# Delta setup of a two-block kernel: work ordered by pairs, block products in whole phases with projection steps between

## The chip, the cores and the metric

The kernel runs on one core of one Trainium2 chip. The metric is the device time of one execution in microseconds. TensorE (PE), VectorE (DVE), ScalarE (ACT), GpSimd (POOL) and SyncE (SP, which only issues DMAs here) run side by side and wait for one another by semaphores.

## What is computed

Four mixers over 256 tokens of width 1024, all in fp32: a gated delta rule layer, an attention layer with a relative bias, a retention layer and a chunked attention layer. The change is in the first, before its output projection:

```
proj = hn @ w_in                                  # q, k, v, z and the gates
qkv  = silu(causal_conv(proj_qkv, conv_w))        # 4 taps
g = cumsum(g); decay = exp(g_i - g_j) below the diagonal, else 0
a_mat = strict_lower((k * beta) @ k.T * decay)
u, w  = solve((a_mat + I), [v * beta, k * beta * exp(g)])
o     = scan over chunks with u, w, q, k, decay
```

In the last two mixers a modulation is needed as well: `mod = silu(c) @ ada_w + ada_b`, 6144 values, read as 24 pairs of columns of 128 (1 MB of weights each).

## The kernel before

**Projections.** Every projection is cut into jobs of 256 columns. A job takes one weight chunk of 1 MB (a job of the third and fourth output projection takes two), which SP loads into `raw` (three buffers: chunk c is issued when the low part of chunk c - 3 is done). ScalarE rounds it to its high part (`high(c)`, two halves, L980), DVE subtracts to get the low part (`low(c)`, two halves, L1382), and PE multiplies three times per tile (high by high, high by low, low by high). `parts(J, s0, s1)` does steps s0 to s1 of the eight steps of job J; a step is six matmuls of 128x256. Two PSUM banks alternate between jobs.

**Delta setup.** Jobs 0 to 7 give keys and queries, 8 to 11 the values, 12 to 15 the gate z. From job 8 on they are cut up and laid between the setup of the delta rule, in an order that is written out by hand on each engine. For each of four pairs of heads p: `decay_rows(p)` spreads the rows of g over the partitions, `masked(p)` adds the causal mask, `products(p, 0)` and `products(p, 1)` make k k' and q k'. ScalarE makes `state_decay(p)` and `decay(p)` (L1108, L1117), DVE multiplies them in `pair_matrices(p)` (L1531 to L1535) into `nt` and `qkd`.

The inverse of the unit lower triangle is then built in seven levels. In levels 0 to 4 `first_products` and `second_products` are 64 block matmuls of 32x32 each (128 rows in the trace), with a ScalarE copy between them (L1154). `take_rows` on DVE puts the results into the triangle (L1552) and transposes it (L1556). Level 5 joins blocks of 32, level 6 blocks of 64. Between the phases PE does four steps of a job, the transposes of the keys (level 1) and of the values (levels 2 to 5), and in levels 5 and 6 a modulation sum. Values that have been transposed are scaled into `vr` by DVE (`take_values`, L1487).

**Modulation.** For pair n DVE multiplies and adds the 1 MB ring of weights (`pair_sums(n)`, L1460 to L1467), PE sums over the partitions (`ada(n)`, two matmuls of one column), DVE adds the bias (`take_mod`, L1473). `ADA_AT[n]` is the job of pair n; the next pair's weights are loaded into the ring three chunks after it. Pairs 0 to 2 are in the setup or just behind it.

**Bias rows.** POOL writes two tables of bias rows to DRAM, each row 32 times (`scr_d` 1 MB and `scr_b` 0.5 MB, L426 and L428), to be read back skewed for the two attention layers.

PE then takes the delta rule's chain (`un_ok` to `o_ok`), the output projection (jobs 16 to 19) and the other mixers, in jobs 20 to 103.

Of the kernel before, what the change touches and what calls it, by code (L numbers as in the profile page):

```python
# [15 lines left out]
P = 128  # L16
# [10 lines left out]
ALU = mybir.AluOpType  # L27
# [35 lines left out]
ADA_AT = [13, 14, 15, 25, 27, 29, 31, 33, 35, 42, 44, 46, 48, 50, 52, 54, 56, 58, 60, 62, 78, 82, 86, 90]  # L63
ADA_EARLY = 3
# [11 lines left out]
def two_blocks(nc, x_in, wts, ada_w, cols_in, const_in, lmask_in, w_ab, rel_b, rel_d, dtab, pos, out,  # L76
               scr_b, scr_d):
    ctx = ExitStack()
    with ctx:  # L79
# [120 lines left out]
        for lv in range(1, LEVELS):  # L200
            if lv == LEVELS - 1:
                turn_order += [f"level{lv}_{g}" for g in range(4)]
            if 2 <= lv <= 5:
                turn_order.append(f"values{lv - 2}")
            if lv >= 5:
                turn_order.append(f"mod{lv - 5}")
# [182 lines left out]
        def _(pool):  # L389
# [35 lines left out]
            pool.wait_ge(nt_ok_sem, 4)  # L425
# [49 lines left out]
        def _(pe):  # L475
# [58 lines left out]
            def ada_after(J):  # L534

                for n in range(ADA_EARLY, ADA_PAIRS):
                    if ADA_AT[n] == (J + 3 if J >= JOB_D else J):
                        if J >= JOB_D:
                            pe.wait_ge(pT_v_sem, 2 * (4 + (J - JOB_D) // 4))
                        pe.wait_ge(mod_ok_sem, n - 2)  # L540
                        ada(n)
# [88 lines left out]
            pe.wait_ge(const_r_sem, 3)  # L630
            decay_rows(0)
# [18 lines left out]
            def first_products(lv, c0):  # L650

                left = left_of(lv) if lv < 5 else lambda v: v
                n = 16 if lv < 5 else 32
                for m16 in range(16):
                    o = slice(c0 + m16 * n, c0 + m16 * n + n)
# [4 lines left out]
            def second_products(lv, c0):  # L660

                n = 16 if lv < 5 else 32
                for m16 in range(16):
                    o, i = slice(c0 + m16 * n, c0 + m16 * n + n), slice(m16 * n, m16 * n + n)
# [7 lines left out]
            parts(9, 4, 8)  # L672
# [7 lines left out]
            for lv in range(1, LEVELS):  # L680
                J = 9 + lv
# [31 lines left out]
                if lv >= 5:  # L713
# [91 lines left out]
            ada(ADA_EARLY - 1)  # L805
# [24 lines left out]
            def attend(J0, pairs, soft0, o0, h_q, h_kv, normed, ready, extra):  # L830
                def turn(i):
                    pe.wait_ge(p_soft_sem, soft0 + i + 1)
                    if soft0 == 0:
                        pe.wait_ge(ss_read_sem, own_ss[0])
                    for hh in range(2):
                        if soft0 == 4 and hh and 1 <= i < 5:
                            pe.wait_ge(mod_ok_sem, 18 + i)
# [126 lines left out]
        def _(act):  # L964
# [155 lines left out]
            state_decay(0)  # L1120
            state_decay(1)
            high(9)
            decay(0)
            decay(1)
            first_tap(8)
            state_decay(2)
            state_decay(3)
            decay(2)
            decay(3)
            high(10)  # L1130
            silu(8)
# [6 lines left out]

            for lv in range(1, LEVELS):
                J = 9 + lv  # L1140
                high(J + 1)
                if lv == LEVELS - 1:
# [7 lines left out]
                else:  # L1150
                    act.wait_ge(x_ok_sem, lv)
                    n = 256 if lv < 5 else 512
                    for k, r in steps_of(lv):
                        m = act.activation(xs32[block_of(r), 0:n], ps[2 + k][block_of(r), 0:n], ACT.Copy)  # L1154
                    m.then_inc(xc_ok_sem, 1)
                    if lv == 5:
                        act.wait_ge(t_ok_sem, 5)
                        act.wait_ge(tt_ok_sem, 5)
                        for i in range(4):
                            m = act.activation(tt[block_of(i), :, block_of(i)], tt32[block_of(i), :, :], ACT.Copy)  # L1160
                        m.then_inc(tt_diag_sem, 1)
                if J - 1 < 12:
                    first_tap(J - 1)
                else:
                    gate_z(J - 1)
                if lv in (2, 3, 4):
                    silu(J - 2)
                if lv >= 2:
                    for p in ((lv - 2,) if lv < 6 else ()):
                        act.activation(qsq[:, 2 * p:2 * p + 2, :], qh[:, 2 * p:2 * p + 2, :], ACT.Square, scale=0.128).then_inc(qsq_ok_sem, 1)  # L1170
# [185 lines left out]
        def _(dve):  # L1356
# [9 lines left out]
            def low(c, halves=range(2)):  # L1366

                if c >= N_CHUNKS:
                    return
                low_only(c, halves)  # L1370
                if c in ADA_AT[ADA_EARLY:]:
                    n = ADA_AT.index(c)
                    if ADA_EARLY < n < 20:
                        take_mod(n - 1)
                    pair_sums(n)
# [104 lines left out]
            def take_values(i):  # L1480

                b, free, n = slot(slot_of_values(i))
                dve.wait_ge(vT_ok_sem, i + 1)
                for c in range(2):
                    for hh in range(2):
                        k = 8 * c + 2 * i + hh
                        m = dve.tensor_scalar(vr[:, 4 * i + 2 * c + hh, :], b[:, (2 * c + hh) * P:(2 * c + hh) * P + P], hc[:, 4, k:k + 1], None, ALU.mult)  # L1487
                m.then_inc(free, 1)

# [47 lines left out]
            low(9)  # L1537
            pair_matrices(0)
            pair_matrices(1)
            conv(8)  # L1540
# [26 lines left out]
            low(10)  # L1567
            for lv in range(1, LEVELS - 1):
                low(10 + lv)
                if lv == 1:  # L1570
# [7 lines left out]
                    dve.wait_ge(ce_sem, 2)  # L1578
                else:
                    take_values(lv - 2)  # L1580
# [4 lines left out]
                if lv <= 3:  # L1585
                    conv(8 + lv)
                if lv == 4:
                    dve.wait_ge(sil_ok_sem, 1)
                    pair_sums(0)
                if lv == 5:  # L1590
                    mod_of_slot(0)
                    pair_sums(1)
            mod_of_slot(1)
            pair_sums(2)
# [141 lines left out]

            add_x(JOB_OUT_A, before_last=lambda: take_mod(ADA_EARLY - 1))

# [31 lines left out]
            def gains_of_c():  # L1770
                for n in range(ADA_EARLY - 1):
                    dve.wait_ge(slot(slot_of_mod(n))[1], slot(slot_of_mod(n))[2] + 1)
                dve.wait_ge(mod_ok_sem, 6)
# [72 lines left out]
            dve.wait_ge(mod_ok_sem, 10)  # L1846
            add_x(JOB_OUT_C, gate=16, before_last=lambda: take_mod(19))
            dve.wait_ge(mod_ok_sem, 18)
# [9 lines left out]
            dve.wait_ge(mod_ok_sem, 22)  # L1858
# [118 lines left out]
```

## Time and profile before

| | us |
|---|---|
| median of 3 runs | 860.55 (859.98 to 864.71) |
| profiled execution | 857.89 |
| its span in the profile | 856.0 |
| TensorE busy in the span | 827.2 (97%) |
| VectorE, ScalarE, GpSimd busy | 602.2, 484.0, 42.0 |
| granted TensorE clock, mean | 0.986 of 2.4 GHz |

The span is the stretch that the profile shows; the profiled execution took 1.9 us more than it. The granted clock of 1.00 is 2.4 GHz, 0.50 is 1.2 GHz. A busy PE is not PE at its peak.

### The profile page before, as it was taken

To read this page: it belongs to the slowest core of one execution; us is meant where nothing else is said; L and a number is where in the kernel's file an instruction comes from. 1 tells how busy PE (TensorE), PEld (TensorE's weight loads), DVE (VectorE), ACT (ScalarE), POOL (GpSimd) and SP (SyncE) were. 2 spreads that over 40 slices of the span, in tenths; PEclk is the share of its full clock that TensorE was granted. 3 is DMA by queue.
4 is the path that set the end of the run, shared out by engine and by line. 5 is a ranking of instruction groups with operands and counts; after the bars stand their busy time and mean duration, and the time that the engine had idled before them with its cause. 6 is when DMAs were issued, how large, how long until landed. Compare 5 with 4: busy or idle time off the path is not lost. (4 is left out here: it accounts for less than half of the span.)

```text
span 856.0 us, 18089 instructions
## 1 busy us (share of the span) xinstructions
PE 827.2 (97%) x7682; PEld 804.6 (94%) x7682; DVE 602.2 (70%) x1058; ACT 484.0 (57%) x746; POOL 42.0 (5%) x63
## 2 busy tenths in 40 slices
PE   6999879899999999999999999998999999999998
PEld 6899878898999999999999999998999999999998
DVE  5785667667887877596888885646678677565662
ACT  4765435445666564564454445345867767777731
POOL 4100000003600000000000000200000000000000
PEclk9999889899999999999999999999999999999999
DMA  7363371261876565447666564793456444434350
GB/s 279 111 242 129 51 188 58 102 221 57 237 236 245 199 244 198 148 154 281 217 234 238 210 244 147 198 289 123 179 197 224 166 156 178 163 119 177 133 188 25
DMA packets 26497, 153.84 MB, mean 180 GB/s; under 512 B 2848, under 2 KB 3376, under 8 KB 12080
## 3 DMA queue, kind: packets, MB, share of 16 engines
q1 hardware_dynamic: 24432, 146.37, 48.3%
q0 software_dynamic: 1984, 6.31, 4.2%
q8 instruction: 61, 1.00, 0.4%
q14 instruction: 20, 0.16, 0.1%
HBM read 150.04 MB, written 2.62 MB: 178 GB/s over the span
## 5 line engine op out<-in xcount | busy, mean ns | idle before, releaser
L1382 DVE TENSOR_TENSOR wlo<-raw,whi 128x1024 fp32r<-128x1024 f32 x224 | 266.1, 1225 | 128.8 <-ACT whi L980 128.8
L479 PE MATMUL ps<-hhi,whi 128*128 128x256 f32 x1024 | 297.3, 290 | 7.4 <-DVE hlo L1408 4.4
L980 ACT ACTIVATE whi<-raw 128x1024 fp32r<-128x1024 f32 x224 | 227.0, 1053 | 126.9 <-PE ps L479 87.5
L479 PE MATMUL ps<-hlo,whi 128*128 128x256 f32 x1024 | 292.6, 286 | 2.7 <-issue 2.7
L479 PE MATMUL ps<-hhi,wlo 128*128 128x256 f32 x1024 | 292.3, 285 | 1.0 <-issue 1.0
L479 PEld LDWEIGHTS ps<-hhi,whi 128*128 128x128 f32 x1024 | 198.7, 194 | 10.7 <-issue 6.4
L479 PEld LDWEIGHTS ps<-hlo,whi 128*128 128x128 f32 x1024 | 198.9, 194 | 3.4 <-issue 2.9
L479 PEld LDWEIGHTS ps<-hhi,wlo 128*128 128x128 f32 x1024 | 198.8, 194 | 1.2 <-issue 1.2
L479 PE MATMUL ps<-ohi,whi 128*128 128x256 f32 x448 | 128.8, 287 | 1.3 <-DVE olo L1427 1.2
L479 PE MATMUL ps<-ohi,wlo 128*128 128x256 f32 x448 | 126.7, 283 | 0.0
L479 PE MATMUL ps<-olo,whi 128*128 128x256 f32 x448 | 126.7, 283 | 0.0
L479 PEld LDWEIGHTS ps<-ohi,whi 128*128 128x128 f32 x448 | 85.9, 192 | 2.4 <-issue 1.6
L479 PEld LDWEIGHTS ps<-olo,whi 128*128 128x128 f32 x448 | 85.9, 192 | 0.5 <-issue 0.5
L479 PEld LDWEIGHTS ps<-ohi,wlo 128*128 128x128 f32 x448 | 85.9, 192 | 0.0
L479 PE MATMUL ps<-arena 128*128 128x256 f32 (+2 forms) x496 | 77.8, 308 | 0.7 <-ACT arena L1343 0.7
L479 PEld LDWEIGHTS ps<-arena 128*128 128x128 f32 (+1 forms) x496 | 70.1, 191 | 7.1 <-issue 3.0
L479 PE MATMUL ps<-whi,hhi 128*128 128x256 f32 x256 | 72.8, 284 | 0.0
L479 PE MATMUL ps<-whi,hlo 128*128 128x256 f32 x256 | 72.4, 283 | 0.0
L479 PE MATMUL ps<-wlo,hhi 128*128 128x256 f32 x256 | 72.4, 283 | 0.0
L1463 DVE SCALAR_TENSOR_TENSOR ada_ring<-ada_ring,sil 128x256 f32<-128x256 f32 x144 | 59.0, 477 | 0.0
L479 PEld LDWEIGHTS ps<-whi,hhi 128*128 128x128 f32 x256 | 49.0, 191 | 0.7 <-issue 0.4
L479 PEld LDWEIGHTS ps<-whi,hlo 128*128 128x128 f32 x256 | 49.0, 191 | 0.3
(221 smaller groups left out, 967.7 us busy)
## 6 DMA issues: line engine op xcount, KB each, us to landing
raw<-weights SPq DMA_DIRECT2D x112, 1024.0 KB, 4.9
ada_ring<-ada SPq DMA_DIRECT2D x24, 1024.0 KB, 5.0
arena<-bias_rows_d POOLq DMA_DIRECT2D x4, 512.0 KB, 15.1
x<-x_t SPq DMA_DIRECT2D x2, 512.0 KB, 4.6
bias_rows_d<-early POOLq DMA_DIRECT2D x1, 1024.0 KB, 12.0
arena<-bias_rows_b POOLq DMA_DIRECT2D x4, 256.0 KB, 7.5
arena<-bias_rows_d POOLq DMA_DIRECT2D x4, 256.0 KB, 17.9
out_t<-x SPq DMA_DIRECT2D x4, 256.0 KB, 2.9
```

The source lines that it names most:

```text
L479: return pe.matmul(o, l, r, start=start, stop=stop, skip_group_check=skip)
L980: act.activation(whi[:, unit % UNITS, :, :], raw[:, c % RAW, 4 * half:4 * half + 4, :], ACT.Copy).then_inc(hi_ok_sem, 1)
L1382: dve.tensor_tensor(wlo[:, unit % UNITS, :, :], raw[:, c % RAW, 4 * half:4 * half + 4, :], whi[:, unit % UNITS, :, :].bitcast(F32), ALU.su ...
L1463: own(dve.scalar_tensor_tensor(out=b, in0=b, scalar=sil[:, k:k + 1], in1=ring[:, :, k - 2, :], op0=ALU.mult, op1=ALU.add))
```

## The change

1. The order of the decay and product matmuls goes by pairs: each mask follows the first product of its pair. ScalarE makes state decay and decay of a pair together.
2. Projection steps are counted by `weave`, which goes on from where it stopped: nine steps before level 0, three behind it, and nine in each of the levels 1 to 6 (four behind the first products, five behind the second). The sum is 66; the last two belong to chunk 16, whose bank the output projection begins anew.
3. ScalarE's and DVE's high and low parts, first taps, silus and gates are placed by level to fit. The low part of chunk 9 stands behind the first two pairs of matrices.
4. The values are scaled into `vr` by ScalarE instead of DVE.
5. One modulation pair is left in the setup (level 6); the two others get the jobs 23 and 66, and the waits and indices follow.
6. The two writes of the bias rows wait for the second first tap instead of the last pair of matrices.

```diff
-ADA_AT = [13, 14, 15, 25, 27, 29, 31, 33, 35, 42, 44, 46, 48, 50, 52, 54, 56, 58, 60, 62, 78, 82, 86, 90]
-ADA_EARLY = 3
+ADA_AT = [14, 23, 25, 27, 29, 31, 33, 35, 42, 44, 46, 48, 50, 52, 54, 56, 58, 60, 62, 66, 78, 82, 86, 90]
+ADA_EARLY = 1
...
-            pool.wait_ge(nt_ok_sem, 4)
+            pool.wait_ge(tap_ok_sem, 2)
             pool.dma_start(scr_d[0:32].rearrange("p h t -> h p t"), fd[:, :].unsqueeze(1).to_broadcast([16, 32, 512])).then_inc(scr_out_sem, 16)
...
+            def weave(n):
+                for _ in range(n):
+                    parts(8 + woven[0] // 8, woven[0] % 8, woven[0] % 8 + 1)
+                    woven[0] += 1
             decay_rows(0)
             decay_rows(1)
             products(0, 0)
+            masked(0)
             products(0, 1)
             products(1, 0)
-            parts(8, 0, 4)
+            masked(1)
+            weave(2)
             products(1, 1)
-            masked(0)
-            masked(1)
-            parts(8, 4, 8)
-            for p in (2, 3):
-                decay_rows(p)
-                products(p, 0)
-                products(p, 1)
-            parts(9, 0, 2)
+            weave(2)
+            decay_rows(2)
+            products(2, 0)
             masked(2)
+            products(2, 1)
+            weave(2)
+            decay_rows(3)
+            products(3, 0)
             masked(3)
-            parts(9, 2, 4)
+            products(3, 1)
+            weave(3)
...
             first_products(0, 256).then_inc(tp_ok_sem, 1)
-            parts(9, 4, 8)
+            weave(3)
...
-                if lv >= 5:
-                    ada(lv - 5, taken(slot_of_mod(lv - 5)))
-                parts(J, 0, 4)
                 if last:
+                    ada(0, taken(slot_of_mod(0)))
+                    weave(4)
...
+                    weave(5)
                 else:
+                    weave(4)
                     pe.wait_ge(xc_ok_sem, lv)
                     pe.wait_ge(u32_ok_sem, lv)
                     second_products(lv, 256 if lv < 5 else 0).then_inc(tp_ok_sem, 1)
-                parts(J, 4, 8)
+                    weave(5)
...
-            ada(ADA_EARLY - 1)
...
             for lv in range(1, LEVELS):
+                if 2 <= lv <= 4:
+                    first_tap(7 + lv)
+                elif lv >= 5:
+                    gate_z(7 + lv)
+                if lv < LEVELS - 1:
+                    high(9 + lv, range(1))
+                    act.wait_ge(x_ok_sem, lv)
...
+                    high(9 + lv, range(1, 2))
+                    if lv >= 2:
+                        take_values(lv - 2)
+                    if lv <= 4:
+                        silu(7 + lv)
+                    if lv == 5:
...
+                        high(15)
...
-            low(9)
             pair_matrices(0)
             pair_matrices(1)
-            conv(8)
+            low(9)
             pair_matrices(2)
             pair_matrices(3)
...
             take_rows(0)
-            low(10)
+            conv(8)
             for lv in range(1, LEVELS - 1):
-                low(10 + lv)
+                if 2 <= lv <= 4:
+                    conv(7 + lv)
+                low(9 + lv)
...
-            mod_of_slot(1)
-            pair_sums(2)
+            low(15)
+            dve.wait_ge(sil_ok_sem, 1)
+            pair_sums(0)
+            mod_of_slot(0)
```

## Rows read from the trace of the kernel before

**Rows 1.** The page: busy us (share of the span) and instructions of PE.

```profile
PE 827.2 (97%) x7682; PEld 804.6 (94%) x7682; DVE 602.2 (70%) x1058; ACT 484.0 (57%) x746; POOL 42.0 (5%) x63
```

**Rows 2.** Windows by stage: length, then busy us of each engine, PEclk, DMA share, GB/s.

```profile
73.30:98.80 25.50, 22.96 (x157) 20.83 (x156) 13.88 (x31) 13.05 (x33) 0.00 (x0) 0.93 0.23 83
98.80:181.00 82.20, 72.45 (x1706) 68.51 (x1707) 56.45 (x116) 35.49 (x60) 1.41 (x2) 0.88 0.48 129
...
200.00:856.00 656.00, 647.60 (x5189) 637.49 (x5188) 465.28 (x795) 377.28 (x560) 27.44 (x33) 1.00 0.55 189
```

**Rows 3.** Waits of PE in the setup, 73 to 181 us: total, times, longest.

```profile
PE ps L479 <- issue: 7.7, 5, 2.7
PE ps L479 <- DVE arena L1535: 2.6, 1, 2.6
PE ps L479 <- DVE ada_sum L1467: 1.3, 1, 1.3
```

**Rows 4.** Windows before one fall of the clock and in two stretches behind falls.

```profile
95.40:98.85 3.45, 0.89 (x12) 0.69 (x10) 2.96 (x7) 3.43 (x9) 0.00 (x0) 1.00 0.00 0
98.85:105.70 6.85, 6.85 (x151) 6.81 (x152) 4.75 (x7) 2.73 (x3) 1.41 (x2) 0.50 0.73 82
...
119.30:126.10 6.80, 6.59 (x149) 6.33 (x150) 5.19 (x11) 3.61 (x8) 0.00 (x0) 0.51 0.58 196
```

**Rows 5.** Timeline of PE: start, us, operation, count, idle before it.

```profile
87.86 2.05 PE L479 MATMUL ps<-arena 128*128 128x128 f32 x16
...
105.94 1.26 PE L479 MATMUL ps<-early,arena 32*32 32x16 f32 x128
...
119.51 0.58 PE L479 MATMUL ps<-hlo,whi 128*128 128x256 f32 x1 [2.69 <-issue]
...
134.41 0.38 PE L479 MATMUL ps<-hhi,whi 128*128 128x256 f32 x1 [0.24 <-DVE early L1449]
...
137.47 0.71 PE L479 MATMUL ps<-early 32*32 32x16 f32 x64
```

**Rows 6.** Timeline of ACT.

```profile
54.66 2.01 ACT L980 ACTIVATE whi<-raw 128x1024 fp32r<-128x1024 f32 x2
57.27 0.63 ACT L1064 ACTIVATE arena<-arena 128x512 f32<-128x512 f32 x1 [0.60 <-DVE arena L1449]
...
78.44 0.64 ACT L1108 ACTIVATE early<-ps 128x256 f32<-128x256 f32 x2
```

**Rows 7.** Timeline of DVE.

```profile
100.87 2.96 DVE L1552 COPY_PREDICATED early<-lmask,ps 32x256 f32<-32x256 uint8 x4 [2.10 <-PE ps L479]
...
154.03 2.46 DVE L1463 SCALAR_TENSOR_TENSOR ada_ring<-ada_ring,sil 128x256 f32<-128x256 f32 x6
...
246.10 2.35 DVE L1382 TENSOR_TENSOR wlo<-raw,whi 128x1024 fp32r<-128x1024 f32 x2
...
543.12 0.87 DVE L1666 SCALAR_TENSOR_TENSOR x<-ps,mod,x 128x256 f32<-128x256 f32 x2
```

**Rows 8.** POOL's write; the software queue in 106 to 110 us; landings, 98 to 130 us.

```profile
99.41 0.71 POOL L426 DMA_DIRECT2D bias_rows_d<-early  x1 [64.58 <-DVE arena L1535]
...
q0 software_dynamic: 101, 0.41, 96.7%
...
raw<-weights SPq DMA_DIRECT2D x1, 1024.0 KB, 17.4
...
bias_rows_d<-early POOLq DMA_DIRECT2D x1, 1024.0 KB, 12.0
bias_rows_b<-early POOLq DMA_DIRECT2D x1, 512.0 KB, 21.9
```

**Rows 9.** DMA queues in 549 to 571 us: packets, MB, share of the engines.

```profile
q1 hardware_dynamic: 522, 3.88, 70.6%
q0 software_dynamic: 530, 1.86, 30.6%
```

**Rows 10.** Waits of ACT, 540 to 580 us.

```profile
ACT whi L980 <- DMA raw<-weights: 10.4, 5, 4.0
```

More of the change, by code:

```diff
@@ L204, in two_blocks @@
                 turn_order.append(f"values{lv - 2}")
-            if lv >= 5:
-                turn_order.append(f"mod{lv - 5}")
+            if lv == 6:
+                turn_order.append("mod0")
         turn_order += [f"sum{i}" for i in range(4)]
@@ L633, in _, with first_products @@
             products(0, 0)
+            masked(0)
             products(0, 1)
             products(1, 0)
-            parts(8, 0, 4)
+            masked(1)
+            weave(2)
             products(1, 1)
-            masked(0)
-            masked(1)
-            parts(8, 4, 8)
-            for p in (2, 3):
-                decay_rows(p)
-                products(p, 0)
-                products(p, 1)
-            parts(9, 0, 2)
+            weave(2)
+            decay_rows(2)
+            products(2, 0)
             masked(2)
+            products(2, 1)
+            weave(2)
+            decay_rows(3)
+            products(3, 0)
             masked(3)
-            parts(9, 2, 4)
-            def first_products(lv, c0):
+            products(3, 1)
+            weave(3)
+            def first_products(lv, c0, between=()):
                 left = left_of(lv) if lv < 5 else lambda v: v
@@ L654, in first_products @@
                 for m16 in range(16):
+                    if m16 in between:
+                        weave(1)
                     o = slice(c0 + m16 * n, c0 + m16 * n + n)
@@ L658, in first_products, with second_products @@
                 return m
-            def second_products(lv, c0):
+            def second_products(lv, c0, between=()):
                 n = 16 if lv < 5 else 32
                 for m16 in range(16):
+                    if m16 in between:
+                        weave(1)
                     o, i = slice(c0 + m16 * n, c0 + m16 * n + n), slice(m16 * n, m16 * n + n)
@@ L836, in turn @@
                         if soft0 == 4 and hh and 1 <= i < 5:
[L837 removed]
+                            pe.wait_ge(mod_ok_sem, 19 + i)
                         if soft0 + i:
@@ L1120, in _ @@
             state_decay(0)
+            decay(0)
             state_decay(1)
+            decay(1)
             high(9)
-            decay(0)
-            decay(1)
+            state_decay(2)
+            decay(2)
+            state_decay(3)
+            decay(3)
             first_tap(8)
[L1126 to L1131, printed above, removed]
             def gate_z(J):
@@ L1137, in gate_z, with take_values @@
                 act.activation(zt[:, 2 * i:2 * i + 2, :], bank(J), ACT.Silu).then_inc(bank_free[J % 2], 1)
-            for lv in range(1, LEVELS):
-                J = 9 + lv
-                high(J + 1)
-                if lv == LEVELS - 1:
+            def take_values(i):
+                b, free, n = slot(slot_of_values(i))
+                act.wait_ge(vT_ok_sem, i + 1)
+                act.wait_ge(ce_sem, 2)
+                for c in range(2):
+                    for hh in range(2):
+                        k = 8 * c + 2 * i + hh
+                        m = act.activation(vr[:, 4 * i + 2 * c + hh, :], b[:, (2 * c + hh) * P:(2 * c + hh) * P + P], ACT.Copy, scale=hc[:, 4, k:k + 1])
+                m.then_inc(free, 1)
+            for lv in range(1, LEVELS):
+                if 2 <= lv <= 4:
[5 more added lines that the diff above has]
+                    act.wait_ge(x_ok_sem, lv)
+                    n = 256 if lv < 5 else 512
+                    for k, r in steps_of(lv):
+                        m = act.activation(xs32[block_of(r), 0:n], ps[2 + k][block_of(r), 0:n], ACT.Copy)
+                    m.then_inc(xc_ok_sem, 1)
+                    high(9 + lv, range(1, 2))
[4 more added lines that the diff above has]
+                    if lv == 5:
+                        act.wait_ge(t_ok_sem, 5)
+                        act.wait_ge(tt_ok_sem, 5)
+                        for i in range(4):
+                            m = act.activation(tt[block_of(i), :, block_of(i)], tt32[block_of(i), :, :], ACT.Copy)
+                        m.then_inc(tt_diag_sem, 1)
+                        high(15)
+                else:
                     for g in range(4):
@@ L1149, in _ @@
                         act.activation(uu[:, 4 * g:4 * g + 4, :], v2(b, P), ACT.Copy).then_inc(free, 1)
[L1150 to L1170, printed above, removed]
+                    gate_z(14)
+                    high(16)
+                if 2 <= lv <= 5:
+                    p = lv - 2
+                    act.activation(qsq[:, 2 * p:2 * p + 2, :], qh[:, 2 * p:2 * p + 2, :], ACT.Square, scale=0.128).then_inc(qsq_ok_sem, 1)
             for p in range(4):
@@ L1372, in low @@
                     n = ADA_AT.index(c)
-                    if ADA_EARLY < n < 20:
+                    if ADA_EARLY < n < 20 and n != 8:
                         take_mod(n - 1)
@@ L1478, in mod_of_slot @@
                 take_mod(n, b, free)
[L1480 to L1488, printed above, removed]
             dve.wait_ge(ones_ok_sem, 6)
@@ L1735, in attend @@
                 finish(pairs - 1)
-            add_x(JOB_OUT_A, before_last=lambda: take_mod(ADA_EARLY - 1))
+            add_x(JOB_OUT_A)
             low(JOB_B + 1, range(1, 2))
@@ L1770, in gains_of_c @@
             def gains_of_c():
-                for n in range(ADA_EARLY - 1):
-                    dve.wait_ge(slot(slot_of_mod(n))[1], slot(slot_of_mod(n))[2] + 1)
-                dve.wait_ge(mod_ok_sem, 6)
+                take_mod(7)
+                dve.wait_ge(slot(slot_of_mod(0))[1], slot(slot_of_mod(0))[2] + 1)
+                dve.wait_ge(mod_ok_sem, 7)
                 scaled_gain(0)
@@ L1845, in _ @@
             finish_c(3, 1)
-            dve.wait_ge(mod_ok_sem, 10)
+            dve.wait_ge(mod_ok_sem, 11)
             add_x(JOB_OUT_C, gate=16, before_last=lambda: take_mod(19))
-            dve.wait_ge(mod_ok_sem, 18)
+            dve.wait_ge(mod_ok_sem, 19)
             scaled_gain(1)
@@ L1857, in _ @@
             attend(JOB_D, 8, 4, A(bias_at, 16, 384), True)
-            dve.wait_ge(mod_ok_sem, 22)
+            dve.wait_ge(mod_ok_sem, 23)
             add_x(JOB_OUT_D, gate=40)
```

16 lines of the change are left out of this document (2 added, 14 removed).

## The prediction

> **What bounds the kernel now.** I first read the page's busy shares: PE is busy for 97% of the span [rows 1]. Next I cut the span into stages. From 200 us on PE is busy for 647.6 of 656 us at full clock; the delta setup, 73.3 to 181.0, is where it is neither (2.5 us idle in the first part, 9.8 us in the second, granted clock 0.93 and 0.88) [rows 2]. The waits of PE there say what the idle time is: 7.7 us under "issue", 2.6 us for the last decay matrices, 1.3 us for the first modulation sum [rows 3]. The windows around the clock's changes show the rest: three times it stands at 1.2 GHz for 6.8 us, each time after PE had waited beside small products (0.9 us busy of 3.45 before the first) [rows 4] (two are shown, the third lies at 156.9 to 163.7). So PE's own order sets the end, and a change here is worth what it removes in idle time and in stretches at 1.2 GHz.
>
> **A model of the setup, tested on the kernel before.** From the timeline of PE [rows 5]: a block of 24 projection matmuls (4 steps of `parts`) takes 3.06 us (134.41 to 137.47), so a step is 0.765; a phase of 128 block products takes 1.19 (1.26 shown) at full clock, 1.9 at half; eight products of 128x128 take 2.05, so one call of `products` is 1.03. The 52 steps after 98.82 make 39.8 us, nine phases and the two of level 5 make 13.2, the transposes, the 64-wide products and the two modulation sums 11.1: 64.1 us, which would end at 162.9. The setup ends at 180.9. The missing 18.0 are 7.7 of issue stalls, 1.5 of other waits, and 8.8, or 2.9 for each of the three times at 1.2 GHz.
>
> **Order by pairs.** The new order begins `masked(0)` right after `products(0, 0)`, at about 77.1. It needs the first state decay, which ScalarE finishes at 78.8 [rows 6]; what stood in that gap, two calls of products, now stands behind it. PE waits 1.8 us. From there I add four masks (0.3 each), seven calls of products, two of decay rows (0.53 each) and nine steps: the first level can start near 95.3, with `nt_ok` 4 reached at 94.5 (the last `decay` is 1.1 us, the last pair of matrices 1.4). Before, it started at 98.8 with 12 steps done: 3.5 us earlier, less 2.3 us for the three steps still to do. The 2.6 us wait goes.
>
> **Levels.** There are nine steps in each level where there were eight, 57 to the end of the setup. Counted, 12 + 54 is 66 steps where jobs 8 to 15 have 64: two surplus steps, 12 matmuls, are paid with 1.4 us. 57 steps make 43.6, the rest 23.9 (one modulation sum less): 67.5 us. To this come waits. After level 0 only three steps (2.3 us) cover the four masked copies of 2.96 us [rows 7]: 0.8. VectorE then has a convolution (2.4), a low part (2.35) and the scaled keys (2.2) before the copies of level 1: 0.7. From level 2 on VectorE has 7.3 us of work (the values went to ScalarE) in a level of 9.9. At level 5 ScalarE now does 1.2 + 1.1 + 1.1 (values) + 2.55 + 2.0 + 0.6 and then the gate of job 13, which job 15 waits for: 9.2 us after the products, where PE arrives after 8.1: 1.1. With 0.2 more the waits are 2.8, and the setup would end at 165.6. I choose this small sum for the values on ScalarE because its four copies have the size of those that VectorE does in 1.12; nothing in the trace lets ScalarE's differ by more than a few tenths.
>
> **What comes back of stalls and clock.** The stalls named issue [rows 3] stand 127 or 128 matmuls apart where one follows another (three such pairs in the timeline; the stall of the first ends at 119.51 [rows 5]). I read them as a fetch of the next piece of program, which from stall's end to stall's end takes 3.7 to 4.1 us, and 5.9 to 7.2 while the bias rows were being written. In the new order I counted on in steps of 127: four of twelve pieces last only 2.3 to 3.6 us. That makes some 5 us of stalls; the bounds are 3 and 8. The clock: the likeliest place for a fall is the wait before level 2 with its first products and a stall behind them, then the waits at levels 5 and 6. I take between one and two falls, 4 us; bounds 0 and 8.8 (as before). So the setup ends at 174.6, 6.3 us earlier: I take 6 us gained, between 2 and 13.
>
> **Bias rows in the first jobs.** The two writes of 1.5 MB move from 99.4 to about 35.0 (the second first tap ends at 34.5, the filled rows at 34.8) [rows 6, 8]. In their old place they took 12.0 and 21.9 us to land, and the weight chunk issued 7.4 us behind them took 17.4 [rows 8]: in 106 to 110 us the software queue held 96.7% of the DMA engines and the weights' queue moved nothing, and from 111 to 122 it still held half. That chunk was not needed for 20 us. In the new place chunk 6 is issued at 41.2, 6.2 us behind the writes; in the same way it would land at about 60. ScalarE takes it at 54.66 in the trace of before, ahead of the silu and the squares of job 4 (0.63 + 0.63) [rows 6], and PE's key sums at 60.02 wait for those squares. So: 59.8 + 2.0 + 1.3 gives 63.2, a wait of 3.2 us, 5.6 if the writes are late by the 2.3 us that chunk 5 still needs. I take 3.5. The lower bound is nothing: the later bias load shares, weights 70.6% and software queue 30.6% [rows 9], and then chunk 6 lands near 50. The upper is 7.6: chunk 5, issued at 34.24, is held as well and its low part, due at 54.2, comes at 61.8. The Trainium skill's page DMA: Bandwidth & Descriptors, section Queues, rings and completion order, says that each engine takes turns between the queues that have work, a packet at a time; by it this term would be nothing. No weights moved in 106 to 110, so this trace speaks against it for these writes.
>
> **Modulation sums at jobs 23 and 66.** Each moves 3.5 us of VectorE (0.6 + 2.46 + 0.42) [rows 7] and 0.4 of PE out of the setup; PE's part is the same in sum. At chunk 23 they stand before the eight low parts of h and the low part of chunk 24: this ended at 248.4, its first half at 247.3, and job 24 begins at 249.3. Now the half comes at 250.9: 1.2 us, and 0.3 again at job 26, whose low part follows the softmax that is 2.5 us later. I take 1.5 (bounds 0.5 and 2.5). At chunk 66 they stand before the update of x at 543.1, whose square on ScalarE is ahead of the high part of chunk 67: low part at 550.5 instead of 546.9, due at 548.1, 2.4 us. And the ring's next MB is now loaded at chunk 69 (about 546.7), not at 65, into 541 to 577 us, where the DMA engines are full and ScalarE already waits 10.4 us for weights [rows 9, 10]. One MB is 2.5 to 5 us there; since the end of this stage hangs on the last weights before too, the two don't add. I take 3.0 (bounds 1.5 and 5).
>
> **Sum.** -6 + 3.5 + 1.5 + 3.0 = +2 us on the profiled execution's 857.9, so 859.9; the median of the runs shown stands 2.7 above that execution, so 862.5. What this kernel's measurement can tell from no change is 0.5%, or 4.3 us.
>
> **Rivals.** (a) The clock does not fall in the new setup and the stalls lie in the waits: 13 us gained, -5, and 852 to 856 by how many of the other terms are paid. For it: the projection steps now stand in every level between the phases, and the longest wait left is 1.8 us. Against it: each of the three falls of before followed such a meeting [rows 4]. It decides from 12.3 us gained in the setup. 0.14. (b) The queues share, the bias rows cost nothing (the page's rule): -1.5, 859. Only with more than 9 us gained in the setup is that faster. 0.23. (c) Chunk 5 is held with chunk 6: +6, 866.6. 0.14. (d) The clock falls three times as before, once after the 1.8 us wait at 77, so that the setup gives 1 to 2 us: +6.5, 867. 0.14. My forecast: 0.35.
>
> **Chances and range.** Faster: all of (a) and 0.07 of (b): 0.21. Slower: (c), (d) and 0.06 of the forecast's own upper end: 0.34. The same: 0.45. The range takes in (a)'s upper half and (d) with a stall more: 854 to 870; the forecast's own is 858 to 866.
>
> **What would show it.** No wait of 2.6 us before the first phase, and a wait of 1.8 near 77; 12 matmuls more on PE; the setup's end between 172 and 178, with issue stalls of 3 to 8 us; the landing time of chunks 5 and 6, and PE waiting at key sums near 60 for ScalarE's squares; a wait for a low part at the start of job 24; waits for low parts in jobs 65 and 67. I am wrong if chunk 6 lands by 50, if the clock is full from 82 to the end of the setup or falls three times in it, or if the low parts of 24, 67 and 70 come in time.

## The result, and the profile after

The changed kernel takes 864.43 us in the median of 20 runs (860.88 to 868.83), the kernel before 860.28 in the same number (854.79 to 865.11). The ratio is 1.0052, with a 95% interval of 1.0029 to 1.0075: slower by half a per cent, just at the edge of what a measurement of this kernel tells from no change. The profiled execution has a span of 862.2 us against 856.0, 6.2 more. The medians are 4.2 apart: the profiled execution of the kernel before (857.89) lies 2.4 below its median, that of the changed kernel (864.05) 0.4 below.

The page of the changed kernel has the 12 surplus matmuls, and 1.2 us more of PE time with them, against [rows 1]:

```profile
PE 828.4 (96%) x7694; PEld 805.9 (93%) x7694; DVE 598.8 (69%) x1042; ACT 487.4 (57%) x762; POOL 41.9 (5%) x63
```

**Where the 6.2 us are.** Four marks on PE cut both traces: the key sums of job 7 (72.43 before, 77.29 after), the first inner products behind the setup (180.88, 177.00), the last sums of x's squares behind job 70 (577.14, 584.74), and the end. The start costs 4.9 us. The setup takes 99.7 us and no longer 108.5, which gives 8.7. The stretch from there to the x sums takes 407.7 and no longer 396.3, which costs 11.5, and 1.4 come back behind it, where PE before waited 1.1 us. 4.9 - 8.7 + 11.5 - 1.4 is 6.2 with the rounding.

The start. POOL writes the bias rows 64 us earlier than in [rows 8]; the software queue in 40 to 44 us, and the landings in 30 to 70 us:

```profile
35.09 0.71 POOL L426 DMA_DIRECT2D bias_rows_d<-early  x1 [0.31 <-POOL early L423]
...
q0 software_dynamic: 101, 0.41, 94.5%
...
bias_rows_d<-early POOLq DMA_DIRECT2D x1, 1024.0 KB, 12.8
...
bias_rows_b<-early POOLq DMA_DIRECT2D x1, 512.0 KB, 23.0
```

In 40 to 44 us the queue of the weights has no row at all, as in 106 to 110 before. Chunk 6 was issued at 41.14; its first packet moved at 45.50, 4.4 us later, where before it was 1.0 us (42.16 after 41.20). From 48 to 55 us the two queues moved side by side, the software queue with 48.3% of the engines and the weights with 37.7%. ScalarE gets chunk 6 at 60.06, where [rows 6] has 54.66, and PE's key sums wait for the squares behind it. The timelines of ACT and of PE, and two windows of PE's clock:

```profile
60.06 2.00 ACT L993 ACTIVATE whi<-raw 128x1024 fp32r<-128x1024 f32 x2 [5.34 <-DMA raw<-weights]
...
62.62 0.63 ACT L1082 ACTIVATE early<-arena 128x512 f32<-128x512 f32 x1
```

```profile
63.30 1.05 PE L479 MATMUL ps<-ones,early 128*128 128x1 f32 x8 [3.17 <-ACT early L1082]
...
83.72 0.80 PE L479 MATMUL ps<-causal_r,ident_r 128*128 128x512 f32 x1 [2.47 <-ACT early L1121]
...
102.25 1.26 PE L479 MATMUL ps<-early,arena 32*32 32x16 f32 x128
...
106.67 1.26 PE L479 MATMUL ps<-early,arena 32*32 32x16 f32 x128 [0.82 <-DVE early L1568]
...
120.23 0.27 PE L479 MATMUL ps<-hhi,wlo 128*128 128x256 f32 x1 [0.68 <-issue]
125.56 0.36 PE L479 MATMUL ps<-early 32*32 32x16 f32 x20 [1.89 <-issue]
```

```profile
65.00:71.00 6.00, 6.00 (x41) 6.00 (x41) 4.18 (x11) 1.50 (x2) 0.00 (x0) 0.75 0.65 246
82.00:88.00 6.00, 4.28 (x18) 4.19 (x19) 1.87 (x5) 3.04 (x10) 0.00 (x0) 0.50 0.00 0
125.50:131.00 5.50, 5.44 (x50) 5.41 (x49) 4.92 (x12) 0.00 (x0) 0.00 (x0) 0.69 0.26 100
```

Behind the wait of 3.17 us the clock falls to half for part of 65 to 71 us; that is the rest of the 4.9. In the setup it falls twice more, once about the wait of 2.47 for the first state decay (82 to 88 us) and once behind the stall of 1.89 (125.5 to 131), where it fell three times before.

The setup from mark to mark, the kernel before first, the changed one second (each an answer of its own trace; the columns are those of [rows 2]):

```profile
72.40:180.90 108.50, 96.22 (x1871) 90.14 (x1870) 70.27 (x148) 49.21 (x93) 1.41 (x2) 0.89 0.41 117
```

```profile
77.30:177.00 99.70, 90.53 (x1878) 84.94 (x1877) 60.71 (x112) 53.02 (x109) 0.00 (x0) 0.95 0.28 97
```

The idle time goes from 12.3 to 9.2 us, and PE is busy 5.7 us less for seven matmuls more, because the clock is 0.95 and no longer 0.89.

Jobs 64 to 68. PE's timeline shows the two waits for low parts; the windows behind each show the clock; DVE and ACT show what was late:

```profile
547.88 0.39 PE L479 MATMUL ps<-ohi,whi 128*128 128x256 f32 x1 [1.96 <-DVE wlo L1409]
...
570.46 0.55 PE L479 MATMUL ps<-ohi,whi 128*128 128x256 f32 x1 [3.23 <-DVE wlo L1409]
```

```profile
545.00:550.00 5.00, 3.04 (x23) 2.83 (x22) 3.40 (x3) 4.41 (x5) 0.00 (x0) 0.93 1.00 219
550.00:555.00 5.00, 5.00 (x34) 5.00 (x34) 1.23 (x2) 0.00 (x0) 0.00 (x0) 0.73 1.02 244
...
570.00:575.00 5.00, 4.54 (x21) 4.57 (x22) 3.42 (x6) 2.53 (x4) 1.84 (x2) 0.50 0.92 352
575.00:580.00 5.00, 5.00 (x38) 5.00 (x37) 2.47 (x3) 1.83 (x2) 0.00 (x0) 0.84 0.61 218
```

```profile
541.26 2.44 DVE L1490 SCALAR_TENSOR_TENSOR ada_ring<-ada_ring,sil 128x256 f32<-128x256 f32 x6
...
544.08 0.87 DVE L1675 SCALAR_TENSOR_TENSOR x<-ps,mod,x 128x256 f32<-128x256 f32 x2
546.60 3.50 DVE L1409 TENSOR_TENSOR wlo<-raw,whi 128x1024 fp32r<-128x1024 f32 x3 [1.65 <-ACT whi L993]
```

```profile
568.00 2.00 ACT L993 ACTIVATE whi<-raw 128x1024 fp32r<-128x1024 f32 x2 [9.15 <-DMA raw<-weights]
```

The first wait is the chain of the prediction: pair 19's sums, the update of x, its square, the high part of chunk 67, its low part. The second is the last weight chunk of the stage, which lands late behind the ring's load (issued at 544.19). The waits are 5.2 us. The clock takes 1.7 us in 545 to 555 (0.07 and 0.27 of 5 us each) and 3.3 us in 570 to 580. That makes 10.2 (0.5 us of idle time at 570 us is counted in both), and from the start of job 64 to the x sums it is 53.6 us where the kernel before needed 43.4, which is 10.2 as well. With the 1.4 us that come back behind the x sums these jobs cost 8.8. The other 1.3 us of the stretch were lost earlier, in jobs 16 to 63.

### The profile page after: what moved, and what is told of

Read it like the earlier page. It is cut to its first block, busy times and chain, and to the rows that moved or that the text cites. A ratio compares the mean times of both kernels' runs of the same rounds, so it can differ in the third digit from the quotient of the medians.

```text
span 862.2 us, 18118 instructions
## 1 busy us (share of the span) xinstructions
PE 828.4 (96%) x7694; PEld 805.9 (93%) x7694; DVE 598.8 (69%) x1042; ACT 487.4 (57%) x762; POOL 41.9 (5%) x63
## 4 chain that ended last, share of the span: by engine, by line
PE 83%; DVE 6%; DMA 5%; ACT 4%; issue 2%; SPq 0%; DVEq 0%; ACTq 0%
PE ps L479 81%; DMA raw<-weights 5%; DVE wlo L1409 1%; ACT whi L993 1%; PE ps L854 1%; DVE early L1568 1%; ACT L982 0%; DVE early L1441 0%; DVE hlo L1435 0%; DVE hlo L1437 0%; DVE arena L1441 0%; DVE early L1476 0%; ACT arena L1182 0%; DVE arena L1476 0%; DVE ada_ring L1490 0%
## 5 line engine op out<-in xcount | busy, mean ns | idle before, releaser
L479 PE MATMUL ps<-ohi,whi 128*128 128x256 f32 x448 | 130.9, 292 | 6.5 <-DVE wlo L1409 5.2
L479 PE MATMUL ps<-ohi,wlo 128*128 128x256 f32 x448 | 128.6, 287 | 0.0
L479 PE MATMUL ps<-olo,whi 128*128 128x256 f32 x448 | 128.6, 287 | 0.0
L479 PEld LDWEIGHTS ps<-ohi,whi 128*128 128x128 f32 x448 | 87.9, 196 | 8.1 <-issue 5.1
L479 PEld LDWEIGHTS ps<-olo,whi 128*128 128x128 f32 x448 | 87.9, 196 | 0.5 <-issue 0.5
L479 PEld LDWEIGHTS ps<-ohi,wlo 128*128 128x128 f32 x448 | 87.8, 196 | 0.0
```

The lines of the kernel that those rows point to most:

```text
L479: return pe.matmul(o, l, r, start=start, stop=stop, skip_group_check=skip)
```

## The experiments

The prediction was near in time, but it had taken the setup's gain for the order's and the bias writes for a loss alone, and the stage of jobs 64 to 68 cost three times its term. Each kernel below is the changed kernel with one edit, unless it says otherwise. Each was timed in five rounds against the kernel before; the ratio is to that kernel (the changed one stands at 1.0052).

**e1, the bias writes in their old place.**

```
-            pool.wait_ge(tap_ok_sem, 2)
+            pool.wait_ge(nt_ok_sem, 4)
```

> The changed kernel with the two bias writes back behind the last pair of matrices. Theory (the writes held weight chunk 6): chunk 6 lands within 6 us of its issue, the wait of 3.17 us at the key sums near 60 goes, and job 7 no longer runs at 1.2 GHz (1.7 us), so the key sums of job 7 start at 72.4 instead of 77.3, 4.9 us earlier. Part of it is given back in the setup, where two fetch stalls get 1.5 to 3 us longer: 2 to 3.5 us faster than the changed kernel in all, ratio to the kernel before about 1.002. Rival (ScalarE's own order makes the key sums late): the wait stays and the time is that of the changed kernel.

867.82 us, ratio 1.0097 (1.0062 to 1.0132): 3 to 4 us slower than the changed kernel and not 2 to 3.5 faster. The start is back (key sums at 60.87 and 73.28), but the setup takes 113.2 us. (Its profiled execution was the slowest of its ten, 873.5.) PE's timeline, then the software queue and the instruction queue in 106 to 110 us:

```profile
112.12 0.94 PE L479 MATMUL ps<-early,arena 32*32 32x16 f32 x55 [8.32 <-issue]
```

```profile
q0 software_dynamic: 242, 0.39, 89.7%
q8 instruction: 1, 0.02, 1.5%
```

For 8.3 us PE stands in the middle of a phase with no semaphore to wait for, while the bias writes hold the DMA engines. In its setup the stalls named issue are 14.0 us, where the changed kernel has 3.7.

What PE waited for can be read from the instruction queue. From 98.5 to 109.5 us the software queue is the only one with packets:

```profile
q0 software_dynamic: 297, 1.05, 87.8%
```

The instruction queue has none there; then one of 16,384 bytes moves from 109.75 to 110.74, and PE goes on at 112.12. It is so with every stall named issue in the setups of all fourteen traces of this case, 48 of them: each ends 1.2 to 1.6 us behind the end of such a packet. And each stands at a fixed place of the program, whatever work lies there: counted in matmuls from the kernel's start, the places are multiples of 127.3 apart (978 in the kernel before and in e1, 1360 in the changed kernel and in e1, 1997 in all fourteen). So these stalls are PE's wait for the next piece of its program, and the bias writes make them longer by holding that piece back.

**e5, the same wait moved in the kernel before, nothing else.**

```
-            pool.wait_ge(nt_ok_sem, 4)
+            pool.wait_ge(tap_ok_sem, 2)
```

> The kernel before with nothing changed but the place of the two bias writes (behind the second first tap). Theory: key sums of job 4 and 5 wait 3.2 us for ScalarE, the key sums of job 7 start 4.9 us later than before; in the setup the stalls of 2.3 and 2.7 us shrink to about 1 each and one fall of the clock may go with them (2.9 us). In all 0 to 3 us slower, ratio 1.000 to 1.003. Rival (the writes cost nothing where they are): the key sums of job 7 stay at 72.4 and the kernel is 2 to 6 us faster than before.

856.80 us, ratio 0.9956 (0.9924 to 0.9989): the one line makes the old kernel faster, where the theory had 0 to 3 us slower. The start costs 7.3 us here (key sums at 64.22 and 79.70; against the changed kernel's 4.9, 1.1 more are a fall of the clock near 20 us, which some executions have, and 1.5 a longer fall behind the wait), and the setup then takes 98.0:

```profile
79.70:177.70 98.00, 88.72 (x1870) 83.00 (x1869) 70.06 (x148) 49.19 (x93) 0.00 (x0) 0.97 0.32 113
```

Put together, the setup from mark to mark is:

| | old order | new order |
|---|---|---|
| bias writes at 98 to 99 us | 108.5 | 113.2 (e1) |
| bias writes at 35 to 36 us | 98.0 (e5) | 97.0 to 102.6 (five executions: the changed kernel and e2, e3, e4, e9) |

Down the columns it is 10.5 us, and 10.6 to 16.2. Along the second row it is nothing that five executions with a spread of 5.6 us can tell. The other three cells are one execution each, e1's the slowest of ten and the two of the old order faster than their medians by 2.4 and 2.5 us. If the whole difference between an execution and its kernel's median lay in the setup, the old order would stand at 110.8 and 100.5 us, e1 at 107.5 and the changed kernel at 100.1. By this estimate the late writes cost 10.3 us in the old order and 7.4 in the new, and the new order gives 0.4 to 3.3 us, which the intervals of about 3 us on each side do not tell from nothing. So the gain in the setup belongs in the main to the bias writes, and the new order has none that is shown, though it has two pairs of modulation sums less to do.

**e6, the bias writes behind level 5** (`pool.wait_ge(t_ok_sem, 6)`; they are issued at 153.0).

> The changed kernel with the bias writes behind the halves of level 5 (near 158 us), where the next weight chunk is not needed for over 20 us and PE has few small products left. Theory: the 4.9 us at the start come back and the setup keeps its 8.7 us, so 4 to 5 us faster than the changed kernel, ratio to the kernel before 0.999 to 1.001. Rival (writes cost the same wherever they lie, by contention with the fetches): stalls in level 6 and behind it take 3 us or more back.

856.33 us, ratio 0.9976 (0.9945 to 1.0008). That is more than the 4 to 5 us expected, and both halves are had: the start of before (61.07 and 73.48) and a setup of 96.6 us. Its issue stalls are 2.6 us, none of them behind the writes, so the rival falls: the writes do not cost the same wherever they lie. The setup ends at 170.1, 6.9 us before the changed kernel's. The stretch behind it is still 407.9 us, with a wait of 6.0 at the last weight chunk in place of 3.2, and 6.7 of the 6.9 us are there at the x sums.

**e7, the masks later.** `masked(0)` stands behind the third call of products and `masked(1)` behind the first two steps.

```
             products(0, 0)
-            masked(0)
             products(0, 1)
             products(1, 0)
-            masked(1)
+            masked(0)
             weave(2)
+            masked(1)
             products(1, 1)
```

> The changed kernel with the first mask behind the third call of products and the second mask behind two steps, nothing else moved. Theory (the 2.47 us wait for the first state decay is the price of putting the mask first, and the clock stays at 1.2 GHz for it): the wait shrinks to under 0.3 us, the first block products start 2 to 4 us earlier against the key sums of job 7, and the kernel is that much faster than the changed one, ratio to the kernel before about 1.002. Rival (decay of pair 0 then comes later and the wait moves to the products of pair 2): the start of the first block products moves by less than 1 us.

861.36 us, ratio 1.0028 (1.0000 to 1.0056). The wait of 2.47 is 0.7, the first block products start 21.3 us behind the key sums of job 7 and no longer 25.0, the clock is full through the whole setup, and the setup takes 93.8 us, less than any of the five in the table. The key sums of job 7 come late in this execution (80.06), so that the spans differ by 3.0. In the medians it is 3 us as well, and the intervals of the two kernels overlap.

**e2, pair 19 at chunk 64 in place of 66** (its ring load goes to 67).

```
-ADA_AT = [14, 23, 25, ..., 60, 62, 66, 78, 82, 86, 90]
+ADA_AT = [14, 23, 25, ..., 60, 62, 64, 78, 82, 86, 90]
```

> The changed kernel with modulation pair 19 at job 64 instead of 66; the ring load of pair 20 then is issued two chunks earlier, before the late bias load begins. Theory (the 8.8 us lost in jobs 64 to 68 come from this pair's place): the waits of 1.96 and 3.23 us for low parts and the two falls of the clock behind them go; 6 to 8 us faster than the changed kernel, ratio to the kernel before 0.996 to 0.998. Rival (the loss comes from the shifted phase of the late bias load, not from the pair): both waits stay.

859.47 us, ratio 1.0007 (0.9977 to 1.0037). That is 4 to 5 us below the changed kernel, where 6 to 8 were expected. Both waits for low parts are gone, and a new one stands earlier, for the low part of the attention's output, which VectorE now does behind the sums (the timelines of PE and of DVE):

```profile
525.10 4.52 PE L479 MATMUL ps<-arena 128*128 128x256 f32 x16 [4.07 <-DVE olo L1454]
```

```profile
519.33 2.46 DVE L1490 SCALAR_TENSOR_TENSOR ada_ring<-ada_ring,sil 128x256 f32<-128x256 f32 x6
...
524.26 0.69 DVE L1454 TENSOR_TENSOR olo<-arena,ohi 128x512 fp32r<-128x512 f32 x1
```

**e3, only the ring's load later** (for pair 20 at chunk 74; pair 19 stays at 66).

```
-  if c == (ADA_AT[n - 1] + 3 if n else 8):
+  if c == ((74 if n == 20 else ADA_AT[n - 1] + 3) if n else 8):
```

> The changed kernel with only the ring load of pair 20 moved from chunk 69 to chunk 74, behind the late bias load. It tells the two causes in jobs 64 to 68 apart. If the ring load fills the DMA engines (my second cause), the wait of 3.23 us for the low part of chunk 70 and the fall behind it go, 4 to 6 us faster than the changed kernel; the wait of 1.96 us for chunk 67 stays. If all comes from the sums on VectorE, both waits stay within 0.5 us.

857.74 us, ratio 0.9973 (0.9941 to 1.0005). The second wait is gone, the first is the same, with the clock behind it (the timeline of PE and a window):

```profile
545.30 0.39 PE L479 MATMUL ps<-ohi,whi 128*128 128x256 f32 x1 [1.96 <-DVE wlo L1409]
```

```profile
545.00:550.00 5.00, 4.70 (x26) 4.71 (x27) 3.65 (x4) 1.83 (x2) 0.00 (x0) 0.66 1.01 256
```

The stretch from the setup to the x sums is 401.7 us instead of 407.7: 6.0 less for one load of 1 MB that is issued 25 us later.

**e4, only pair 19's sums later on VectorE** (behind the low parts of chunks 67 and 68; the ring's load stays at 69).

```
-  if c in ADA_AT[ADA_EARLY:]:
+  if c in ADA_AT[ADA_EARLY:] and c != 66:
...
+  if J0 == JOB_OUT_C and n == 1:
+      take_mod(18)
+      pair_sums(19)
```

> The changed kernel with only the sums of pair 19 on VectorE moved from before the update of x after job 64 to behind the low parts of chunks 67 and 68; the ring load stays at chunk 69. If the order on VectorE is the first cause, the wait of 1.96 us for the low part of chunk 67 goes (and with it the fall behind it, 1.5 us) and the wait of 3.23 us for chunk 70 stays or grows to 5: 0 to 3 us faster than the changed kernel. If the ring load is the cause of both waits, both stay.

864.51 us, ratio 1.0069 (1.0037 to 1.0101): nothing gained in the median. The first wait is gone and the second is longer:

```profile
575.00 0.55 PE L479 MATMUL ps<-ohi,whi 128*128 128x256 f32 x1 [6.51 <-DVE wlo L1409]
```

The stretch is 406.2 us, 1.5 less. While the last chunk is late, what is saved ahead of it is waited for there.

**e9, e3's and e4's edits together.**

> Changed kernel with both edits of the two runs before: the ring's load for pair 20 is issued at chunk 74 and pair 19's sums stand behind the low parts of chunks 67 and 68. Theory (each of the two waits of jobs 65 and 67 has its own cause, and the cost of the stage is the waits and the clock falls behind them): the ring's load was the larger part (its removal alone gave 6 to 8 us), and the sums only move a wait from chunk 67 to the last weight chunks (their removal alone gave nothing). With the load out of the way the sums no longer stand between a late chunk and its low part: both waits go, and the time is 1 to 3 us below the ring edit alone, 855 to 857. Rival (the sums cost VectorE 3.5 us wherever they stand in these jobs, and the end of the stage hangs on VectorE's low parts): within 1 us of the ring edit alone, 857 to 859, with one wait of 2 us at a later chunk.

856.88 us, ratio 0.9983 (0.9955 to 1.0011). No wait of 1 us or more is left from 540 to 577 us, and the stretch is 398.0 us: 9.7 less than the changed kernel, where the two edits alone gave 6.0 and 1.5. The median is 0.9 us below e3's, which is less than its interval; the trace agrees with the theory, and the medians decide nothing between it and the rival.

**e10, the values on VectorE again.** The four scaled copies of `take_values` are VectorE's `tensor_scalar` as before the change, ahead of `take_rows` in levels 2 to 5.

> Changed kernel with the values copied by VectorE again, everything else as in it. Theory (ScalarE is the late one at level 5, by 1.35 us, and VectorE's copies of levels 1 to 4 have room for 1.12 us more): the wait at level 5 goes, the other levels wait 0 to 1.1 us longer where VectorE has a low part and a convolution; the sum within 1.5 us of the changed kernel, 863 to 866, so that the move of the values is worth nothing that can be measured. Rival (VectorE is what sets each level of the new order, and the move is what made the order possible): each of levels 2 to 4 waits about 1 us and the clock falls behind one or two of them; 867 to 872.

863.36 us, ratio 1.0049 (1.0014 to 1.0085), the same as the changed kernel's. The wait at level 5 is 0.35 us, not 1.35, and the other levels wait 1.4 us where the changed kernel's wait 1.1. The setup takes 97.9. The rival, that this move made the order possible, falls.

**e8, e6 + e7 + e2 and two surplus steps fewer** (`weave(3)` at the end).

> The changed kernel with four edits together: bias writes behind level 5, pair 19 at job 64, the first masks later, and no surplus steps. Theory: 4.5 + 7 + 2 + 1.4 = 15 us faster than the changed kernel, ratio to the kernel before 0.986 to 0.991. Rival (the gains share the same falls of the clock and fetch stalls, so they don't add): 6 to 9 us faster than the changed kernel, ratio 0.994 to 0.998.

850.69 us, ratio 0.9901 (0.9867 to 0.9935): by the ratios 13.0 us faster than the changed kernel, where the theory said 15 and the rival 6 to 9. Alone e6, e2 and e7 gave 6.5, 3.9 and 2.1 us by their ratios, 12.5 in sum, so with the two surplus steps gone the gains add within their intervals.

**e11, the same with e3's edit in place of e2's.**

> The version with the bias writes behind level 5, the masks later and two surplus steps fewer, but with pair 19 left at chunk 66 and the ring's load for pair 20 issued at chunk 74 (in place of the pair at chunk 64). Theory (the pair at chunk 64 costs a wait of 4.1 us for the output's low part that the ring edit does not have, and keeps clear of the two waits of jobs 65 and 67; the ring edit leaves only the wait of 2 us): 1 to 2 us below the version with the pair at 64, 848 to 850. Rival (the two are alike, both end with the last weight chunk): within 1 us of it, 850 to 852.

846.45 us (six runs), ratio 0.9872 (0.9830 to 0.9913). It lies below the expected 848 to 850. Its profiled execution was the slowest of the six (850.8), and even so its span of 849.0 is 1.4 below e8's; the stretch takes 400.2 us against e8's 403.1. By the trace the edit to the ring is the better of the two, and the intervals of e8 and e11 overlap.

**e12, e11 with e4's edit as well.**

> The fastest version so far (bias writes behind level 5, masks later, two surplus steps fewer, the ring's load for pair 20 at chunk 74) with pair 19's sums moved behind the low parts of chunks 67 and 68 as well. In the profiles, the stretch from the first inner products behind the setup (near 171 to 181 us) to the last sums of x's squares (near 577) takes 407.7 us in the changed kernel, 401.7 with the ring edit, 398.0 with ring and sums edits together, 396.3 in the kernel before. Theory (the stretch is set by PE's order and its two waits there, whatever the setup did before it): 396 to 398 us here too, where the version without the move of the sums takes 400.2, so 2 to 4 us less in the span, 845 to 847, and a median of 843 to 846. Rival (what the stretch gives back is taken elsewhere, or the medians can't tell it): the same 400 us and a median of 846 to 848.

845.74 us (six runs), ratio 0.9844 (0.9809 to 0.9879), the fastest kernel here, though its median can't be told from e11's. The profiled execution was its fastest, with a span of 841.5. The stretch takes 398.4 us (e11: 400.2), so 1.8 of the 7.5 us between the two spans (e11's slowest execution against e12's fastest) are the edit's; 5.2 are the setup, which is the same code in both (e12 first, e11 second):

```profile
73.20:165.60 92.40, 86.93 (x1866) 81.43 (x1865) 60.24 (x112) 53.03 (x109) 1.42 (x2) 0.98 0.39 104
```

```profile
73.60:171.30 97.70, 91.50 (x1867) 85.69 (x1866) 60.40 (x113) 53.23 (x109) 1.42 (x2) 0.93 0.39 103
```

## Why the prediction was right or wrong

The forecast was 862.5 us, its own range 858 to 866, and the median is 864.4. Against the kernel before it was +2; the medians have +4.2, the trace +6.2.

**The setup: 6 forecast, 8.7 measured, with the wrong cause.** The parts that could be read off the trace came as worked out: 57 + 9 steps and 12 matmuls more, waits of 0.82 and 0.31 after levels 0 and 1 (0.8 and 0.7 forecast), 1.35 at level 5 (1.1), 3.7 us of stalls (5), the setup's end at 177.0, in the forecast's 172 to 178. The step that failed is the reading of what comes back of stalls and clock. I took the three falls of before for the meeting of waits with small products, which the order would mend, and the bias writes only for a load on the weights' queue. e5 has the old order with its phases unmended, and without the writes in it the setup takes 98.0 us. The trace of before had said as much: pieces of program took 3.7 to 4.1 us, and 5.9 to 7.2 while the bias rows were being written. I used that row for a part of the stalls and did not ask what the whole setup would be without the writes. That the setup's gain came out near its term is luck: the order, which the term was for, has 0.4 to 3.3 us by the estimate under e5.

**The wait for the first state decay** was 2.47 us, not 1.8, and the clock stood at half around it. In e7 the wait is 0.7 and the clock stays full, so both were a cost of putting the mask first.

**The bias rows in the first jobs: 3.5 forecast, 4.9 measured.** The mechanism held to the tenth: chunk 6 at 60, key sums at 63.2 against 63.30, 3.17 us of wait. What was left out is the fall of the clock behind the wait. Rival (b), that the bias rows cost nothing, falls: chunk 6 landed 18.9 us after its issue, and even its first packet moved only 4.4 us after it. The prediction's reading of 106 to 110 us was too strong, though: the weight chunk was issued only at 106.85, and its first packet moved at 110.57. The Trainium skill's page DMA: Bandwidth & Descriptors, section Queues, rings and completion order, lets each engine take turns between queues, a packet at a time. The 94.5% of the software queue, with chunk 6 waiting from 41.14 to 45.50, are against it for the first of the two writes; from 48 us on the queues did share, and the chunk was late all the same. Rival (c) falls as well, since the low part of chunk 5 was not late.

**Job 23 and the jobs to 63: 1.5 forecast, 1.3 measured.** The only wait in 240 to 260 us is one of 0.77 at the start of job 24, for which 1.2 were forecast; at job 26 there is none. The trace names it a stall of issue, but it is none of the stalls for the program: it is not at one of their places, and PE starts 0.10 us behind the end of the first half of chunk 24's low part (246.44, 246.54), in the changed kernel and in all eleven others with the sums at chunk 23. So the mechanism was right here. The other 0.5 us are not traced to a place.

**Jobs 64 to 68: 3.0 forecast with bounds 1.5 and 5, 8.8 measured.** This is the term that was mis-sized, by more than the rest together. The two waits were both named, with 2.4 us and 2.5 to 5, and came with 1.96 and 3.23. Two things about them were wrong. No fall of the clock was counted for them, though the falls cost 5.0 us, as much as the waits. And the ring's MB was priced too low: where the sums are out of its way (e4) the wait for the last chunk is 6.51 us. "The two don't add" held only in small part. Against the stretch of e9, 398.0 us, which has neither, the sums alone cost 3.7 us (e3), the load alone 8.2 (e4), and the two together 9.7, which is 2.2 less than their sum: the last chunk takes back some of what is saved ahead of it. So e3's and e4's edits together give 9.7 of the 11.5.

So a gain forecast 2.7 too small stood against losses forecast 1.4 and 5.8 too small, and the sum was 4.2 us too low on the profiled execution and 2.2 in the medians. Without the errors' different signs it would have been farther off. Rival (a) falls (the clock fell twice in the setup), though e7, with both masks later, does what it said: the clock is full, and the setup takes 14.6 us less than before. Rival (d), with three falls and 1 to 2 us gained, falls as well.

What stays open: what the other parts of the change do by themselves. The sixth part was taken alone (e5) and the fourth taken back (e10); the even nine steps in each level, the two modulation pairs moved out and the two surplus steps were never tested one at a time. Nor do the runs show why the clock falls behind a wait in one execution and not in another.

## What to carry to other kernels

A large background write is not free because nothing waits for its data: place it where neither a weight chunk nor the program of a busy engine is due behind it, and try it alone first. Here one line gave 0.4% on the old kernel, and in the new order two other places for it were 1.2% apart. Price a short wait of PE at one and a half to two times its length if the clock may fall behind it: here 3.17 us cost 4.9, 1.96 cost 3.7 and 3.23 cost 6.5, while 1.98 in e11 cost no more than itself. Two delays in one stage don't give back their lengths one by one: the later one takes back what the earlier one gives, so remove the last first.

## What was not expected of the hardware

- PE stood still for 8.32 us within a phase of block products, with no semaphore to wait for, while POOL's writes to DRAM held 89.7% of the DMA engines (e1). With the writes elsewhere the longest such stall of the changed kernel is 1.9 us. A 16 KB packet of the instruction queue ended 1.4 us before PE went on.
- The same wait for the low part of chunk 67 was followed by a granted clock of 0.66 in e3 (1.96 us of wait) and by 1.00 in e11 (1.98 us; the timeline and the window):

```profile
542.16 0.39 PE L479 MATMUL ps<-ohi,whi 128*128 128x256 f32 x1 [1.98 <-DVE wlo L1409]
```

```profile
540.00:545.00 5.00, 3.02 (x25) 2.85 (x24) 4.12 (x4) 3.69 (x4) 0.00 (x0) 1.00 1.00 246
```

- Five executions of one and the same setup code took 97.0 to 102.6 us, with a clock of 0.96 in the shortest and 0.90 in the longest. A single profile of this stage shows less than it seems to.
